# Attention of the first block by pairs of heads, its four kinds interleaved by column block

## The reference, cut to what matters

```
nsa:  s = q.k * scale;  p = softmax(s, causal);  o = g1 * p@v_slc + g2 * p@v_win + g0 * p_cmp@v_cmp
fox:  s = q.k * scale + cum_f[t] - cum_f[key];  p = softmax(s, causal);  o = p@v
sb:   z = q.k * scale;  sp = softplus(z) where key < t
      a = exp(log_sigmoid(z) - sum of the later sp);  o = a@v
gates = sigmoid(h @ w_gate + b_gate)                      # 4 x 1024 columns
mixed = sum over the branches of gates * (y_branch @ w_branch);   x = x + mixed @ w_out
```

## Time and profile before

| | |
|---|---|
| time, median of 3 | 2626.25 us (2625.92 to 2627.27) |
| profiled execution, span | 2632.6 us |
| TensorE busy | 2434.9 us (92%) |
| weight loads busy | 1885.3 us (72%) |
| VectorE busy | 1178.4 us (45%) |
| ScalarE busy | 1031.8 us (39%) |
| DMA, mean rate | 130 GB/s |
| mean granted TensorE clock | 0.958 |

### The profile page before, as it was taken

How to read it: one execution, slowest core, us unless ns; L and a number is a source line. 1 busy time by engine, 2 the same in 40 slices (tenths; PEclk the granted TensorE clock), 3 DMA queues, 4 the chain that set the end, 5 groups by cost and what they waited for, 6 DMA issues and landing times. The chain is left out here.

```text
span 2632.6 us, 31895 instructions
## 1 busy us (share of the span) xinstructions
PE 2434.9 (92%) x13191; PEld 1885.3 (72%) x13191; DVE 1178.4 (45%) x1672; ACT 1031.8 (39%) x1684; POOL 16.3 (1%) x23
## 2 busy tenths in 40 slices
PE   5999999989978999999989979889899999998998
PEld 4897667759868897667859855444688887454897
DVE  4465444235424464443335431456334335265456
ACT  3443224326424433225136424672422331344453
POOL 0000000000000000000000000000000000100000
PEclk9998999999998999999989979899999999999999
DMA  7433444644516425444535532101222223122352
GB/s 210 173 129 128 160 161 176 201 151 160 180 68 204 163 81 192 160 160 160 192 113 191 192 137 90 47 1 60 74 88 87 92 88 84 50 96 80 130 191 81
DMA packets 197137, 341.13 MB, mean 130 GB/s; under 512 B 45955, under 2 KB 60734, under 8 KB 196862
## 3 DMA queue, kind: packets, MB, share of 16 engines
q1 hardware_dynamic: 194300, 334.68, 36.2%
q0 software_dynamic: 944, 3.47, 0.4%
q10 hardware_dynamic: 1746, 0.89, 0.1%
HBM read 335.88 MB, written 3.15 MB: 129 GB/s over the span
## 5 line engine op out<-in xcount | busy, mean ns | idle before, releaser
L261 PE MATMUL bank<-hT_high,ring_low 128*128 128x256 f32 (+1 forms) x1520 | 461.2, 303 | 0.0
L556 PE MATMUL bank<-work,ring 128*128 128x256 f32 x1536 | 361.6, 393 | 8.4 <-DMA ring<-w_in 4.9
L556 PEld LDWEIGHTS bank<-work,ring 128*128 128x128 f32 x1536 | 295.5, 196 | 60.5 <-issue 20.5
L261 PEld LDWEIGHTS bank<-hT_high,ring_low 128*128 128x128 f32 x1520 | 291.8, 192 | 12.4 <-issue 0.5
L260 PE MATMUL bank<-ring_low,hidden_high 128*128 128x512 f32 x640 | 254.4, 397 | 0.0
L949 ACT ACTIVATE work<-bank 128x512 f32<-128x512 f32 (+6 forms) x260 | 121.9, 485 | 231.1 <-PE bank L262 175.7
L248 DVE TENSOR_TENSOR ring_low<-ring,half_high 128x2048 fp32r<-128x2048 f32 x64 | 146.4, 2292 | 136.8 <-ACT half_high L241 136.8
L556 PE MATMUL bank<-work 64*128 64x128 f32 (+8 forms) x1032 | 192.3, 336 | 4.6 <-DVE work L1266 4.4
L260 PE MATMUL bank<-hT_low,half_high 128*128 128x512 f32 (+1 forms) x512 | 176.9, 345 | 11.6 <-DVE hT_low L2300 8.2
L949 ACT ACTIVATE work<-bank,work 128x256 f32<-128x256 f32 (+1 forms) x200 | 88.2, 458 | 245.5 <-PE bank L556 155.7
L241 ACT ACTIVATE half_high<-ring 128x2048 fp32r<-128x2048 f32 x64 | 121.7, 1908 | 154.3 <-PE bank L262 154.3
(11 more groups left out here) (207 smaller groups left out, 4312.0 us busy)
## 6 DMA issues: line engine op xcount, KB each, us to landing
ring<-w_ff SPq DMA_DIRECT2D x32, 2048.0 KB, 8.1
ring<-mlp_w SPq DMA_DIRECT2D x32, 2048.0 KB, 8.2
ring<-w_in SPq DMA_DIRECT2D x30, 2048.0 KB, 9.4
ring<-w_ada SPq DMA_DIRECT2D x24, 2048.0 KB, 9.0
ring<-w_branch SPq DMA_DIRECT2D x6, 2048.0 KB, 14.3
ring<-w_in SPq DMA_DIRECT2D x32, 256.0 KB, 4.2
ring<-w_out SPq DMA_DIRECT2D x4, 2048.0 KB, 7.7
ring<-gqa_w_qkv SPq DMA_DIRECT2D x3, 2048.0 KB, 15.9
```

Source lines behind the costliest of these rows:

```text
L261: nc.tensor.matmul(out, a[1], b[0], start=False, stop=False)
L556: return nc.tensor.matmul(out, lhsT, rhs, start=start, stop=stop)
```

## The change

The 32 jobs become 16 pairs m: the two heads of one column block and one kind. Their order is slc, win, fox, sb for c = 0, then the same for c = 1, 2, 3. In `scores` the products of the two heads alternate (row half, other row half) into two banks, then come fox's 8-row products of both heads, then the masks of both. In `output` the products alternate between the column halves of one bank. A step has two fillers and handles one pair: filler, `turned(m-1)`, `scores(m)`, filler, `output(m-1)`. Where the pair before is sb, the second filler is put ahead of `scores`. ScalarE and VectorE follow the same order; VectorE now does the sigmoid of the first filler ahead of the row maxima; ScalarE does both Ln of an sb pair behind one another. The number of products, their shapes and the bytes moved stay. The diff, cut to TensorE's part and the main lines of the others:

```diff
     for c in range(HALF_HEADS):
-        for g in range(2):
-            jobs += [("slc", c, g), ("win", c, g)]
-    jobs += [("fox", h // 2, h % 2) for h in range(8)]
-    jobs += [("sb", h // 2, h % 2) for h in range(8)]
+        jobs += [(kind, c, e) for kind in ("slc", "win", "fox", "sb") for e in range(2)]
     NJ = len(jobs)
+    PAIRS = NJ // 2
+    soft_jobs = [j for j in range(NJ) if jobs[j][0] != "sb"]
+    sb_jobs = [j for j in range(NJ) if jobs[j][0] == "sb"]
+    soft_count = {j: n + 1 for n, j in enumerate(soft_jobs)}
+    sb_count = {j: n + 1 for n, j in enumerate(sb_jobs)}
+    halves_of = [slice(0, HD), slice(HD, P)]
...
+            def scores(m):
+                kind, c, _ = jobs[2 * m]
+                ps = [SC.claim(pe, f"s{2 * m + e}") for e in range(2)]
                 if kind == "sb":
+                    for e, r in enumerate(halves_of):
+                        mm(ps[e][:, 0:S], sbk[r, c, 0:P], sbq[r, c, :], True, False)
+                    for e, r in enumerate(halves_of):
+                        mm(ps[e][:, S:S + P], sbk[r, c, P:S], sbq[r, c, P:S], False, False)
+                    for e in range(2):
+                        mm(ps[e][:, 0:P], M("ident"), M("strict"), False, False)
+                        mm(ps[e][:, S:S + P], M("ident"), M("strict"), False, True).then_inc(SC.full, 1)
...
                 for t in range(TT):
+                    n, at = (t + 1) * P, t * P
+                    for e, r in enumerate(halves_of):
+                        if kind == "fox":
+                            mm(ps[e][:, at:at + n], fxq[r, c, t * P:(t + 1) * P], fxk[r, c, 0:n], t == 0, False)
+                        else:
+                            mm(ps[e][:, at:at + n], nsaT[r, c, t * P:(t + 1) * P], nsaT[r, 4 + (kind == "win"), 0:n], t == 0, False)
+                if kind == "fox":
+                    for e in range(2):
+                        for t in range(TT):
+                            n, at = (t + 1) * P, t * P
+                            mm(ps[e][:, at:at + n], head_sel[0:8, 2 * c + e, :], fox_row[0:8, 0:n], False, False)
+                for e in range(2):
+                    mm(ps[e][:, 0:P], M("ident"), M("causal"), False, False)
+                    mm(ps[e][:, S:S + P], M("ident"), M("causal"), False, True).then_inc(SC.full, 1)
+            def turned(m):
+                for e in range(2):
+                    j = 2 * m + e
+                    if jobs[j][0] == "sb":
+                        ps = SC.bank(f"s{j}")
+                        pe.wait_ge(sb_soft, sb_count[j])
...
+                    ps = PT.claim(pe, f"p{j}")
+                    pe.wait_ge(prob_ready, soft_count[j])
...
+            def output(m):
+                kind, c, _ = jobs[2 * m]
                 group = "nsa" if kind in ("slc", "win") else kind
                 name = f"o_{group}{c}"
                 first, last_of = (kind != "win"), (kind != "slc")
+                ps = OT.claim(pe, name) if first else OT.bank(name)
                 if kind == "slc":
+                    PT.taken(pe, f"pc0{c // 2}", f"pc1{c // 2}")
+                    for e, r in enumerate(halves_of):
+                        mm(ps[r, 0:S], vc[0:N_CMP, e, :], pcT[e][0:N_CMP, c, :], True, False)
                 if kind == "sb":
+                    SC.taken(pe, f"s{2 * m}", f"s{2 * m + 1}")
                 else:
+                    PT.taken(pe, f"p{2 * m}", f"p{2 * m + 1}")
+                heads = [slice((2 * c + e) * HD, (2 * c + e + 1) * HD) for e in range(2)]
+                v = {"slc": [vs[:, :, r] for r in halves_of], "win": [vw[:, :, r] for r in halves_of],
+                     "fox": [fxv[:, :, h] for h in heads], "sb": [sbv[:, :, h] for h in heads]}[kind]
+                for e, r in enumerate(halves_of):
+                    mm(ps[r, 0:S], v[e][:, 0, :], probT[:, e, 0:S], kind in ("sb", "fox"), False)
+                for e, r in enumerate(halves_of):
+                    last = mm(ps[r, P:S], v[e][:, 1, :], probT[:, e, S:S + P], False, last_of)
+                if last_of:
                     last.then_inc(OT.full, 1)
...
+            for m in range(PAIRS + 1):
+                if m < PAIRS:
+                    filler(2 * m)
+                if m >= 1:
+                    turned(m - 1)
+                later = m >= 1 and jobs[2 * m - 2][0] == "sb"
+                if later and m < PAIRS:
+                    filler(2 * m + 1)
+                if m < PAIRS:
+                    if m == 2:
+                        PROJ.taken(pe, "fc", "fv0", "fv1", "fk0", "fk1")
+                    scores(m)
+                if m == 0:
                     turn_compressed()
-                if 1 <= i <= NJ:
-                    turned(i - 1)
-                if i >= 2:
-                    output(i - 2)
+                if not later and m < PAIRS:
+                    filler(2 * m + 1)
+                if m >= 1:
+                    output(m - 1)
...
+            def scores(m):
+                if jobs[2 * m][0] == "sb":
+                    for e in range(2):
+                        ps = SC.arrived(act, f"s{2 * m + e}")
+                        link(f(sb_u[:, e], ps[:, 0:3 * P], ACT.Abs))
+                        link(f(sb_u[:, e], sb_u[:, e], ACT.Exp, scale=-1.0))
+                    for e in range(2):
+                        f(sb_u[:, e], sb_u[:, e], ACT.Ln, bias=one).then_inc(sb_log, 1)
+                    return
...
+            for m in range(PAIRS):
+                filler(2 * m)
+                later = m >= 1 and jobs[2 * m - 2][0] == "sb"
+                if later:
+                    filler(2 * m + 1)
+                scores(m)
+                if not later:
+                    filler(2 * m + 1)
```

More of the change, by code:

```diff
@@ L811, in scores @@
[L811 to L831, removed]
@@ L869, in _, with filler @@
+                if last_of:
+                    last.then_inc(OT.full, 1)
+            def filler(i):
+                w = W.arrived(pe, f"gate{i // 4}")
+                ps = PROJ.claim(pe, f"g{i}")
+                if i == 0:
+                    pe.wait_ge(hT_whole, 1)
+                for k in range(KD):
+                    last = mm(ps[:, 0:S], w[:, k, i % 4 * P:(i % 4 + 1) * P], hT[:, k, :], k == 0, k == KD - 1)
+                last.then_inc(PROJ.full, 1)
                 if i in (2, 3):
@@ L897, in _ @@
                     PROJ.taken(pe, "gyT0", "gyT1")
-                    OT.taken(pe, "o_sb2", "o_sb3")
+                    OT.taken(pe, "o_fox3", "o_sb3")
                 for f in range(KD // 2):
@@ L1091, in _, with filler @@
             copy(fox_row[0:8, :], ps[0:8, 0:S]).then_inc(PROJ.free("fc"), 1)
[L1093 to L1097, removed]
+            def filler(i):
+                ps = PROJ.arrived(act, f"g{i}")
+                f(gates[:, i, :], ps[:, 0:S], ACT.Exp, scale=-1.0, bias=cols[:, ROW_GATE + i:ROW_GATE + i + 1])\
+                    .then_inc(PROJ.free(f"g{i}"), 1)
                 if i in (2, 3):
@@ L1108, in _ @@
                     take(f"ada{ada_steps.index(i)}", ada_p)
[L1109 to L1131, removed]
+            def turned(m):
+                for e in range(2):
+                    j = 2 * m + e
+                    if jobs[j][0] == "sb":
+                        act.wait_ge(sb_later, sb_count[j])
+                        ps = SC.arrived(act, f"s{j}")
+                        f(probT[:, e], ps[:, 0:3 * P], ACT.Exp).then_inc(SC.free(f"s{j}"), 1)
+                    else:
+                        ps = PT.arrived(act, f"p{j}")
+                        copy(probT[:, e], ps[:, 0:3 * P]).then_inc(PT.free(f"p{j}"), 1)
@@ new lines, in output @@
+            def output(m):
+                kind, c, _ = jobs[2 * m]
+                if kind != "slc":
+                    group, at = {"win": ("nsa", 0), "sb": ("sb", 4), "fox": ("fox", 12)}[kind]
+                    ps = OT.arrived(act, f"o_{group}{c}")
+                    copy(yT[:, at + c, :], ps[:, 0:S]).then_inc(OT.free(f"o_{group}{c}"), 1)
+            for m in range(PAIRS + 1):
+                if m < PAIRS:
+                    filler(2 * m)
+                if m >= 1:
+                    turned(m - 1)
+                later = m >= 1 and jobs[2 * m - 2][0] == "sb"
+                if later and m < PAIRS:
+                    filler(2 * m + 1)
+                if m < PAIRS:
+                    scores(m)
+                if not later and m < PAIRS:
+                    filler(2 * m + 1)
+                if m >= 1:
+                    output(m - 1)
```

105 lines of the change are left out of this document (44 added, 61 removed).

## The result

| | time, median | lowest to highest | ratio to the kernel before, 95% interval |
|---|---|---|---|
| before, 4 runs beside it | 2626.76 us | 2625.92 to 2631.81 | 1 |
| changed, 4 runs | 2542.86 us | 2541.26 to 2547.44 | 0.9679 (0.9665 to 0.9693) |
| changed again, 5 runs in a later lot | 2541.01 us | 2539.95 to 2545.08 | 0.9679 (0.9664 to 0.9693) |

The change takes 83.9 us off, where 87.8 were forecast (2538.5 us). The profiled execution has a span of 2539.4 us and took 2541.26, the fastest of the four; the time of a run is about 1.8 us above its span.

The account below looks back on a forecast made before the run. The prediction took TensorE, busy 98% of the attention stages, as the bound. Parts, sb waits, stage ends and clock summed as -86.2 + 8.4 - 2 - 8 = -87.8, from 2626.25 to 2538.5 us, range 2522 to 2564.

Parts of the forecast that it names:

- the parts: TensorE's savings in scores, outputs, transposes and fillers: 10.8 us per column block, 86.2 us for 8 in two layers.
- 8.4 - 2 = 6.4: TensorE waits: six sb waits of 1.4 us add 8.4; shorter waits at the stage ends take off 2.
- the 0.3 us for the new neighbours of each pair: Transposes and fillers get neighbours of like array shape: 0.3 us saved per pair, between 0 and 0.4.
- Overlap of halves: In scores and outputs, products on different array halves overlap fully: a pair costs what one head cost.
- Changes of shape: On TensorE each change of the array's shape costs some 0.15 to 0.2 us; slc score four, fox score six.
- The wait behind sb pairs: TensorE waits 1.3 to 1.4 us for ScalarE's filler Exp, three pairs per layer: +8.4 us.
- 8-row products one behind the other: In fox scores both heads' 8-row products share rows and columns, so they don't overlap: 1.46 us per pair.
- Transfers and the softmax chain: In the stage, tiles and the pair's softmax arrive in time for TensorE: no wait, nothing added.
- The clock term: Most of 12 us lost to low clock around fox steps goes: -8 us, between -12 and +10.
- the same 6.4 us: The median of the runs is 6.4 us below the profiled span; same difference taken off the forecast span of 2544.8.
- rival 4: In the stage a bank or tile gates each pair some 5 us, +90 for +8: about 2626 us, chance 0.02.
- rival 1: Sb waits of 2 to 3 us each, each letting the clock drop 3.4 to 6.8 us: about 2562, chance 0.09.

Follow-up runs that it names:

- x2: Changed kernel with the scores head after head, the first head's masks between them, outputs still in turn: 2575.14 us, ratio 0.9799 to the kernel before.
- x5: Changed kernel with the two heads' outputs on either side of the filler in 30 of 32 pairs: 2567.35 us, ratio 0.9778 to the kernel before.
- x6: Kernel before, no heads paired; within each head row-half products first, then fox's 8-row products, then both masks: 2608.73 us, ratio 0.9934.
- x4: Changed kernel with ScalarE taking an sb pair's second filler (and adT) ahead of the two Ln, last pair unchanged: 2532.60 us, ratio 0.9641 to before.
- x7: x4 plus fox's 8-row products of the second head on another row group, from a second copy of the gates: 2529.04 us, ratio 0.9626 to before.
- x3: Changed kernel with kinds in the old order, slc and win by column block, then four fox pairs, four sb pairs: 2548.07 us, ratio 0.9697 to before.
- x1: Changed kernel with the first head's products before the second's, not alternating, in scores and outputs: 2542.46 us, ratio 0.9677 to the kernel before.
- the second lot: Later timing lot: changed kernel again, unchanged, five runs, 2541.01 us; kernel before beside it, nine runs, 2627.49 us.

## Why the prediction was right, point by point

The mechanism was right: the halves overlap, the changes of shape pay, and the wait stands where it was put. That the sum came so near (87.8 against 87.4 in the stages of the two profiles) is partly luck, since two of its terms were off by about 7 us each in opposite directions: the parts too large, the clock too small.

- **The sum, term by term.** TensorE's busy time in the two stages fell from 509.8 to 415.7 us, by 94.1. Low clock inside the stages covers 36.7 us before and 6.6 after, half of which is lost, except where TensorE was idle: 18.0 and 3.3. So the work at full clock fell by 94.1 - 14.7 = 79.4, where the parts had 86.2. TensorE's idle time in the stages rose by 6.7 (10.0 to 16.7), where 8.4 - 2 = 6.4 were forecast: 7.9 behind the sb pairs and about 1.6 at the start of the stages, less 2.6 at their end. The clock gave 14.7 in this pair of profiles, where 8 were forecast.
- **Where the parts were too large.** Taken by shape of pass, start to start without waits and with low clock halved (my estimate from the records of both profiles): the scores fell by 45.6 us, forecast 46.5; the outputs by 28.6, forecast 30.1; fillers, transposes and sb sums by 5.3, forecast 32 x 0.3 = 9.6. The step that was mis-sized most is the 0.3 us for the new neighbours of each pair.
- **Overlap of halves.** Right, for rows and for columns, at the price read from the second block. Scores apart cost 32.7 us (x2), outputs apart 26.3 (x5). The rule of the Trainium skill (TensorE: Matmul & The Clock Gate, Part 3, The mechanism) that a weight load overlaps a running matmul only on other rows did not hold here: in x5 four column-half passes are busy as long as eight in the changed kernel. The prediction quoted only this sentence of the section, which also lets a load go ahead into a background weight buffer; so the section as a whole does not speak against the outputs. The slc pair's compressed product, for which I had no row, covers its twin as well (12 passes busy 1.45 us, where the 6 of one head were busy 1.43).
- **Changes of shape.** Right: 0.3 us for an slc or win head and 0.5 for a fox head, 18.8 us in all as a part alone (x6). With x2 and x5 these are 77.8 us that were taken apart by experiment, of the 84 to 86.5 that the change brings. They are differences to two different kernels, each with its own waits and its own clock, so their sum is a check on the size and no exact account.
- **The wait behind sb pairs.** Right in place, cause and size (1.32 read against 1.3 to 1.4), shown by x4. What I had only under a rival is a part of its price: a stretch of low clock followed one of three such waits in layer 0 and none in layer 1.
- **8-row products one behind the other.** Right, 1.50 for 1.46; x7 shows it was the shared rows, since on other rows they take 0.86.
- **Transfers and the softmax chain.** Right: no wait of TensorE for `prob` or for a tile at any pair. The first filler of each stage waits for its tile, 2.7 and 3.4 us; it did before (2.3 and 2.6), ahead of where the stages are measured.
- **What was missing.** At the start of the stage the first pair claims both score banks at once, and the second is freed by VectorE's work on the compressed scores. I had not looked for a wait there. The lines of layer 0 and layer 1, changed kernel:

```profile
243.14 0.93 PE L559 MATMUL bank<-work 64*128 64x128 f32 x8 [0.64 <-DVE work L1367]
968.66 0.93 PE L559 MATMUL bank<-work 64*128 64x128 f32 x8 [2.38 <-DVE work L1367]
```

Another 0.34 us stands ahead of the second transposes in each layer; before, these waits were 0.75 and 1.36. Layer 0 waits less because its first filler ran at low clock and came late: it is busy 5.25 us, in layer 1 3.69. In x4 it is the other way round in layer 1, a slow first filler (5.38) and a wait of 0.65. A low clock in the first filler is thus paid for by a shorter wait behind it and costs next to nothing. The stages were 217.0 and 215.4 us for 214 each; layer 0 holds the stretch of low clock, layer 1 the longer wait.

- **The clock term.** Mis-sized. The prediction counted four stretches of low clock, 23.9 us, in fox steps and the step behind them. There are four more in the stages of the same profile, 12.8 us: two near the start of layer 0, one at the start and one at the end of layer 1 (columns as in the earlier trace rows):

```profile
237.98:241.39 3.41, 3.41 (x10) 2.70 (x9) 1.88 (x8) 1.35 (x3) 0.00 (x0) 0.50 1.05 404
248.22:251.63 3.41, 3.41 (x10) 2.69 (x9) 2.83 (x6) 0.66 (x4) 0.00 (x0) 0.50 1.02 391
1006.40:1009.40 3.00, 2.98 (x7) 2.46 (x8) 0.91 (x4) 2.02 (x4) 0.00 (x0) 0.50 1.05 405
1265.40:1268.40 3.00, 2.23 (x10) 1.39 (x9) 0.00 (x0) 1.09 (x4) 0.00 (x0) 0.50 1.03 418
```

After, only one stretch at the start of layer 0 (237.2 to 240.4) and the one at 346.2 are left. The stretches under a first filler, at 238.0, 1006.4 and 237.2, cost little by what the waits behind them show. What keeps the clock up in the changed kernel no run tests; x3, which groups the fox pairs again, has none among them either. The two profiles also differ in luck: that of the kernel before is at the slow end of its runs (its span of 2632.6 means a time of about 2634.4, and of 18 later runs one was slower), that of the changed kernel the fastest of its four. Profile to profile the gain is 93.2, forecast 87.8; median to median it is 83.9. I took the same 6.4 us off both kernels to get from span to median; the changed kernel's median lies 3.5 above the span of its profile. By the mean clocks of the second lot (0.961 of about 2626 us, 0.965 of 2539) low clock lasts long enough to cost at most 102 and 89 us, so at most about 13 us of the median's gain are the clock's. How much of them it really is stays open, since mean clocks count idle time too.

- **Slips of the prediction that change nothing.** Under rival 4, 5 us for each of 32 pairs would be 160 us, not 90; 90 takes 2.8 each. Under rival 1, 7.1 of 9.7 us are 73%, not 70.

## What to carry to other kernels

Where heads of 64 dimensions leave half of the matrix engine idle, put the products of two of them next to each other, one on each row half into two banks, or one on each column half of one bank: the pair then costs what one did. Count the changes of tile shape in a sequence as well, about 0.15 us each here (x6), and sort a step's products by shape even where nothing can run beside anything. When TensorE's share falls, walk the in-order engines once more for what a filler's release is queued behind: moving one Exp ahead of the two Ln and their table loads, at six places, brought 9.9 us. And add up a forecast's terms against the profile afterwards, even where the total is right: here two misses of 7 us hid each other.

## What was not expected of the hardware

- Two products written one head after the other ran fully beside each other (x1): the second head's first pass started 13 to 14 ns behind the first head's, past a product of the first head that had not begun. The alternation in the source was not needed.
- Products of 8 rows at partitions 0 and 64 covered each other completely, 8 passes in 0.86 us (x7), so here a contraction of 8 rows gained as much from a second copy of its rows as a head of 64 does.
